# One-hot routing rows in one VectorE instruction, and the low part of u on GpSimd, in a hybrid encoder step with PEER experts

## What is computed

```python
q = (xb @ wq).reshape(nb, PEER_HEADS, 2, PEER_DKEY // 2)
s = jnp.einsum('nhpd,hpkd->nhpk', q, sub_keys)           # 8 heads, 2 sides, 128 keys
sv, si = lax.top_k(s, 16)
cand = (sv[:, :, 0, :, None] + sv[:, :, 1, None, :])     # 16 x 16 pairs
cidx = (si[:, :, 0, :, None] * 128 + si[:, :, 1, None, :])
fv, fi = lax.top_k(cand, 16)
eidx = jnp.take_along_axis(cidx, fi, axis=-1)            # 16 of 16384 experts per head
g = jax.nn.softmax(fv, axis=-1)
act = jax.nn.gelu(einsum('nhkd,nd->nhk', expert_u[eidx], xb))
out = jnp.einsum('nhk,nhkd->nd', g * act, expert_v[eidx])
```

## Time and profile before

| | us |
|---|---|
| median of 3 runs | 2014.8 (2012.8 to 2019.0) |
| span of the profiled execution | 2013.1 |
| busy PE / DVE / ACT / POOL | 1914.5 / 1366.2 / 885.0 / 917.6 |
| search stage, steps 2 to 19 | 677 to 778 |
| steps 20 to 29 | 778 to 836 |
| steps 30 to 78 | 836 to 1145.5 |
| steps 79 to 119 | 1145.5 to 1373.4 |
| steps 120 to 127 | 1373.4 to 1414.4 |
| expert stage | 1414.4 to 1995 |

### The profile page before, as it was taken

The page is one execution under the profiler, slowest core; times in us unless marked ns, Lnnn a source line. Parts: engine busy times, 40 slices in busy tenths (PEclk is TensorE's granted clock), DMA queues, the critical chain, the costliest instruction groups (busy, mean ns, idle before and its releaser), DMA issues. The chain is left out here.

```text
span 2013.1 us, 32547 instructions
## 1 busy us (share of the span) xinstructions
PE 1914.5 (95%) x11569; PEld 1816.0 (90%) x11569; DVE 1366.2 (68%) x2638; ACT 885.0 (44%) x1929; POOL 917.6 (46%) x792
## 2 busy tenths in 40 slices
PE   7999989998798999899999899999999999999998
PEld 6978878888797999898999899999999999999997
DVE  3133455666514599798999777776578777778775
ACT  4031022224313346577877688883333333333333
POOL 4433232422324358789999977763022222222210
PEclk8999999999898999999999899999999999999999
DMA  7621169987532245898999799999799999999982
GB/s 173 113 60 53 43 181 242 267 269 240 170 75 74 70 148 180 251 271 255 285 284 282 242 309 314 325 306 308 241 350 336 341 353 325 353 340 337 350 303 97
DMA packets 325341, 478.80 MB, mean 238 GB/s; under 512 B 37532, under 2 KB 250012, under 8 KB 321852
## 3 DMA queue, kind: packets, MB, share of 16 engines
q1 hardware_dynamic: 287740, 341.63, 55.2%
q0 software_dynamic: 36864, 134.23, 20.4%
q10 hardware_dynamic: 576, 0.85, 0.1%
HBM read 391.52 MB, written 83.96 MB: 236 GB/s over the span
## 5 line engine op out<-in xcount | busy, mean ns | idle before, releaser
L1467 PE MATMUL ps<-x_high,split_high 128*128 128x416 f32 x1024 | 373.0, 364 | 10.2 <-DVE split_low L1454 6.9
L1467 PE MATMUL ps<-x_high,split_low 128*128 128x416 f32 x1024 | 363.8, 355 | 0.0
L1467 PE MATMUL ps<-x_low,split_high 128*128 128x416 f32 x1024 | 362.2, 354 | 0.0
L2097 PE MATMUL ps<-hid_high,split_high 128*128 128x416 f32 x1024 | 358.9, 350 | 1.5 <-PEq L1680 1.5
L2097 PE MATMUL ps<-hid_low,split_high 128*128 128x416 f32 x1024 | 358.8, 350 | 0.0
L2097 PE MATMUL ps<-hid_high,split_low 128*128 128x416 f32 x1024 | 358.8, 350 | 0.0
L1657 POOL TENSOR_SCALAR area<-iota_row,chosen 128x128 f32<-128x128 f32 x360 | 330.1, 929 | 2.6
L1336 POOL DMA_INDIRECT gathered_rows<-in_peer_v_dram,gathered_index x128 | 134.5, 1051 | 419.2 <-DVE gathered_acc L1373 342.4
L2040 ACT CAST split_high<-area 128x1024 fp32r<-128x1024 f32 x127 | 133.3, 1049 | 383.5 <-PE ps L2097 382.7
L2068 DVE TENSOR_TENSOR split_low<-area,split_high 128x1024 fp32r<-128x1024 f32 x127 | 155.6, 1225 | 135.2 <-ACT split_high L2040 135.2
L1467 PEld LDWEIGHTS ps<-x_high,split_high 128*128 128x128 f32 x1024 | 195.1, 190 | 16.0 <-DVE split_low L1454 8.5
(11 more groups left out here) (301 smaller groups left out, 3938.8 us busy)
## 6 DMA issues: line engine op xcount, KB each, us to landing
area<-in_peer_v_dram SPq DMA_DIRECT2D x128, 512.0 KB, 5.8
u_nat<-in_peer_u_dram SPq DMA_DIRECT2D x392, 128.0 KB, 5.7
routing<-dense SPq DMA_DIRECT2D x26, 1024.0 KB, 6.3
area<-hidden SPq DMA_DIRECT2D x128, 208.0 KB, 8.0
hidden<-gelu_out SPq DMA_DIRECT2D x124, 208.0 KB, 4.5
w_raw<-in_w_in_dram SPq DMA_DIRECT2D x44, 512.0 KB, 5.8
mv_nat<-in_peer_u_dram SPq DMA_DIRECT2D x120, 128.0 KB, 3.5
u_nat<-turned_u SPq DMA_DIRECT2D x30, 512.0 KB, 3.7
```

What stands on the lines that cost most here:

```text
L1467: ins = self.nc.tensor.matmul(self.k.ps[:, b, 0:N], w[:, b, kk, :], x[:, kk, 0:N], start=(kk == 0 and p == 0), stop=(kk == KD - 1 and p == 2))
L2097: ins = nc.tensor.matmul(ps[:, kk, 0:N], v[:, b, kk * P:(kk + 1) * P], h[:, b, :], start=(n == 0 and p == 0), stop=(n == P - 1 and p == 2))
```

## The change

All batches of `first` are now made by DVE, in its step behind the sort's pieces and ahead of the dots, each batch with a single `tensor_tensor` over four frames: the index row is read four times, each pick 128 times (two broadcast inputs, 128x512 out). POOL makes none. The low part of u is POOL's from tile 2 to the last. `Plan.on_vector` and its semaphore are gone. Steps, batches, sort pieces, dots and fetches stand in the same steps as before.

```diff
-        sorted_by = self.final[-1] + 2
-        self.on_vector = [b for n in sorted(self.routing) for b in self.routing[n] if n >= sorted_by][1::3]
...
-    hidden.lent = range(2, plan.final[2] + 3)
+    hidden.lent = range(2, P)
...
-    vector_first_ready = sem("vector_first_ready")
-
-    def first_rows(eng, b, ready):
-
-        eng.wait_ge(pick_out, turns(plan.turned_for(b)))
-        after(eng, routed, b - AREAS + 1)
-        for f in range(FEW):
-            c = plan.column(b) + f
-            ins = eng.tensor_scalar(first[:, b % AREAS, f, :], iota[:, :], chosen[:, 0, c:c + 1], None, ALU.is_equal)
-        ins.then_inc(ready, 1)
+    def first_rows(dve, b):
+
+        dve.wait_ge(pick_out, turns(plan.turned_for(b)))
+        after(dve, routed, b - AREAS + 1)
+        c = plan.column(b)
+        nc.vector.tensor_tensor(first[:, b % AREAS], bcast(iota[:, :], 1, FEW), bcast(chosen[:, 0, c:c + FEW], 2, P), ALU.is_equal
+                                ).then_inc(first_ready, 1)
...
-                for b in plan.routing.get(n, []):
-                    if b not in plan.on_vector:
-                        first_rows(pool, b, first_ready)
...
-                lent = sum(i <= b for i in plan.on_vector)
-                if b in plan.on_vector:
-                    pe.wait_ge(vector_first_ready, lent)
-                else:
-                    pe.wait_ge(first_ready, b + 1 - lent)
+                pe.wait_ge(first_ready, b + 1)
...
                 for b in plan.routing.get(n, []):
-                    if b in plan.on_vector:
-                        first_rows(dve, b, vector_first_ready)
+                    first_rows(dve, b)
```

## The result

The changed kernel takes 2026.6 us (median of 5 runs, 2021.8 to 2030.4) beside 2015.3 us for the kernel before on the same chip: ratio 1.0056, 95% interval 1.0031 to 1.0081, 11.3 us more. A second set of runs gave 2024.0 beside 2016.2 us, ratio 1.0049 (1.0026 to 1.0073). So it is slower, as forecast, but by 8 to 11 us instead of 25.

A forecast was written before the change was run, and what follows sets the result against it. VectorE, shut out by POOL's 2.40 us subtractions, was taken to bound steps 30 to 78. Terms +22 + 0 + 3 + 0 = +25 us on 2014.8 gave 2039 us; range 2022 to 2052 for the forecast alone, chance 0.48.

The forecast's parts named there:

- Steps 20 to 29: Search steps of 58.0 us before: POOL's freed subtractions against VectorE's added one-hots and blocking; 0, from -4 to +5 us.
- Steps 79 to 119: Search steps without sort: TensorE's pace holds, though fetches now stand behind POOL's subtraction; +3 us, from 0 to +14.
- the reckoned loop of 14.2 us: Steps 79 to 119: fetch, landing, dot, transpose, high and low part take 14.2 us against three steps of 16.35.
- The rival with the gathered rows: Landings above 9.3 us make the loop longer than three steps: 2055 to 2065 us; chance 0.09 for 2053 and more.
- Steps 120 to 127: Last search steps, without a batch: POOL's low part leaves 0.41 us of slack; 0, from -4 to +4 us.
- Steps 30 to 78: Search stretch of 309.5 us before: POOL's subtractions shut VectorE out, giving 332 us, +22.
- the 256 us: VectorE's busy time alone in steps 30 to 78: 282.2, less 61.9 of subtractions, plus 36.0 of one-hots.
- break-even at 1.09: Steps 30 to 78: blocking per step, in us, at which the stretch stays 309.5 us: (309.5 - 256) / 49.
- an even exchange: Rival: POOL often waits for VectorE's dot itself, blocking about 1.1 us per step; 2009 to 2021 us, chance 0.14.
- its two additions: Steps 30 to 78: five two-input sort pieces split by the subtraction, 5.5 us each; nine subtractions pushed back, 6 us.
- 31 pieces end before POOL does: Steps 30 to 78: in 31 sort-piece steps VectorE waits until POOL ends, 4.84 us after the transpose began; 150.0 us.
- the first rival: POOL's subtraction hides under transpose and sort as VectorE runs ahead; 1977 us, or about 1990 with sort ends blocked; chance 0.29.

The follow-up runs named there:

- the quarters: Changed kernel with POOL's low part in four instructions of 128x256 instead of one of 128x1024; 2027.7 us, ratio 1.0092.
- the one-hots alone: Kernel before with only the one-hot rows moved to VectorE in one instruction per batch, low part as before; 2010.8 us, ratio 0.9976.

## Why the prediction was wrong

*Steps 20 to 29*: 0 forecast (-4 to +5), -0.8 and -0.9 measured. Right. *Steps 79 to 119*: +3 (0 to +14) forecast, 0 to -3 measured; the reckoned loop of 14.2 us against 16.35 was wide enough. The rival with the gathered rows did not come in the changed kernel, but the quarters show how near it stands. *Steps 120 to 127*: 0 forecast, -0.4 to -1 measured.

*Steps 30 to 78*: +22 forecast (332 us), 318.5, 310.4 and 310.1 measured, +5 in the mean. The mechanism was right: VectorE became the bound by being shut out, as the one-hots alone and the quarters show. The size was not: VectorE is busy 314.1 and 306.4 us in two profiles, over the 256 us that I had for it without blocking. That is 58 and 50 us, 1.19 and 1.03 us per step, where I had put 1.55, with break-even at 1.09. The 256 was itself too high, since VectorE's 282.2 busy us of before hold waiting beside POOL's compares (dots of 1.30 us, low parts of 1.26; with no compares there they take 1.22 and 1.18). In the run of the one-hots alone VectorE has 242 us without its low parts (299.6 less 57.9), or 249 if the time in which a low part overlaps its neighbours is left to these. Over them the blocking is 57 to 72 us, 1.2 to 1.5 per step, and the break-even moves up with it. What happened in the stretch lies near the rival that I called an even exchange, and gave 0.14. Two steps of the sum failed:

| 49 steps, transpose to transpose, us (shut out: one-hot over 1 us, dot over 2 us) | after | after, again | by the rule |
|---|---|---|---|
| one-hot shut out (25 / 22 steps) | 175.6 | 152.9 | 175.6 / 150.9 |
| a dot shut out (9 / 9) | 69.4 | 67.0 | 62.9 |
| neither (15 / 18) | 71.8 | 89.5 | 80.2 / 105.0 |
| sum | 316.8 | 309.3 | 318.8 |

"The rule" is the prediction's sum with 4.84 us for every sort piece and without its two additions. It gives 318.8. The first failure is these additions, 13 us: 7.6 for pieces with two inputs and 6 for subtractions pushed back. Only 4 to 7 us of that show, in the steps where a dot was struck: POOL shuts VectorE out once per step, and in no step of the two profiles were a one-hot and a dot both struck. The second failure is "31 pieces end before POOL does": I took VectorE to be late in all of them. In 6 steps with a sort piece (35 to 39 and 54; with 42 to 46 it is 11 in the second profile) VectorE had caught up: ScalarE came late to the high part, in half of these steps behind the gelu of the product ahead, the subtraction began 4.1 to 6.6 us into the step instead of 2.4, and nothing was shut out. In 3 and 2 more steps it struck the sort piece. The late start is the first rival, for a part of the stretch; how long that part lasts differs between executions, and with it the stretch. The price of a single shut-out step was nearly right, 6.42 us for 6.65: behind POOL's end 0.47 us of the one-hot is left, not 0.66.

*What the sum did not have*: +6 us at the end of the stage, for which it had no term. I had followed the loop's fetches past the subtraction, but not the three that close POOL's list. The profile of before had what was needed: POOL's last fetch ended at 1401.83, and TensorE waited only 1.53 us between the stages. That such a fetch holds the stage's end for 6 us after it stands in no row of before; that it had been moved behind the last low part could be read from the list of POOL's instructions.

So +5 and +6, less 3 from the other stretches, make 8 of the 8 to 11 us. The sign came out right by luck. The main term that I had was four times too large, and in the runs the search without the late fetches can't be told from the kernel before: 2015.6 us, in the even exchange's 2009 to 2021. What made the kernel slower is the term that the sum did not have. That 2026.6 lies in the range, and even in the 2022 to 2052 of the forecast alone, is luck in the same way.

*The signs named*: the stretch of some 330 us did not come. POOL's subtractions near 2.4 us (median 2.41, mean 2.54) and the transpose as releaser of the high part (35 of 49 times) came; TensorE waited for the one-hot 1.4 us each, but 25 times, not in most steps; the one-hot's median stayed at 0.69 us where I wanted one well above 0.7. A median tells nothing where half are disturbed. The mean, 1.39, is below the 1.5 that I had named as one half of the first rival's sign; the other half, the high part waiting for TensorE, came only in the few steps above, through ScalarE's list, so that sign did not decide.

## What to carry to other kernels

When work moves to GpSimd beside VectorE, place it in time, not in sum: put VectorE's two-input instructions (and its single-input compares) ahead of GpSimd's long one and leave transposes and top-8 instructions beside it; here, with the late fetches out of the way, that order took the kernel from 2015.6 to 2006.9 us, 9 us below the kernel before. Add the blocking once per instruction that shuts others out, not once per instruction that could be hit, and take the busy time that it is added to from a run in which nothing blocks. And follow every instruction that ends up behind the moved work to the end of its list: here a last indirect fetch issued late held the border to the next stage.

## What the runs showed of the hardware that was not expected

- A stage in which GpSimd issued an indirect fetch late ended late: the next stage's first matmul came 6.0 to 6.8 us after the end of the last fetch, in five profiles of four kernels; without a late fetch it came 1.0 to 1.1 us after the last gelu. The landing of that fetch lies 1.3 to 1.4 us ahead of the matmul in the four profiles that record it. Which engine waits for the landing, no run shows.
- After those 5.85 us without matmuls the granted clock was 0.50 for 3.6 us, and 24 of TensorE's matmuls took 6.61 instead of 4.59 us; after 1.53 us it was 1.00.
- VectorE's compare with one large input was shut out by GpSimd's subtraction (2.14 against 0.94 us for four), the top-8 instructions were not (eight MAX8 in 1.51 us under a subtraction of 2.41, 1.50 in the kernel before), nor the transposes (1.24 us on average in both kernels).
- GpSimd's subtraction of a quarter takes 0.74 us, not 0.60: four quarters cost 0.57 us more than one piece before any waiting.
